# Turning activations to features with in-place 32x32 transposes and SBUF-to-SBUF DMAs, in three more places instead of TensorE

## The reference

```
h = h + concat(sgu, shortconv, conformer, pool of rms(h) @ w_in) @ w_out
h = h + (silu(rms(h) @ w_gate) * (rms(h) @ w_up)) @ w_down      # 2048 -> 5632 -> 2048
h = h + sigmoid(rms(h) @ w_ple_gate) * (p @ w_ple_proj)
x = rms(h, final)
q, k, v, gate = split(rms(x) @ swa_w_in)                        # 32 query heads, 4 key heads of 64
o = attention with window 128, bias table and sinks, after a norm of q and k
out = x + (o * silu(gate)) @ swa_w_out
```

## Time and profile before

| what | us |
|---|---|
| median of 3 runs | 1449.11 (1448.94 to 1449.32) |
| the profiled execution's own time | 1450.04 |
| its span | 1448.1 |
| TensorE matmul busy | 1441.9 (6655 instructions) |
| DVE busy | 981.4 |
| ScalarE busy | 697.1 |
| GpSimd busy | 50.4 |
| DMA traffic | 274.03 MB, mean 189 GB/s |

### The profile page before, as it was taken

One profiled execution on the slowest core, in us unless ns is written; L12 is line 12 of the kernel. 1 busy time (PEld: TensorE's weight loads), 2 busy tenths in 40 slices (PEclk: granted clock), 3 DMA queues, 4 the chain that ended last, 5 costly groups with the idle time before them and its releaser, 6 DMA issues.

```text
span 1448.1 us, 18176 instructions
## 1 busy us (share of the span) xinstructions
PE 1441.9 (100%) x6655; PEld 1194.7 (83%) x6655; DVE 981.4 (68%) x1364; ACT 697.1 (48%) x924; POOL 50.4 (3%) x52
## 2 busy tenths in 40 slices
PE   9999999999999999999999999999999999999999
PEld 7888888888888888888888888888888888888887
DVE  5599977886666654566765546769798567665553
ACT  7444564554444433444443344445555566564432
POOL 2000010000000000000000000000000212200000
PEclk9999999999999999999999999999999999999999
DMA  9665556566665556666555666655565745444462
GB/s 332 220 189 175 175 184 220 192 191 190 201 192 197 191 191 197 193 190 195 193 190 192 198 190 194 196 185 179 191 203 175 236 155 171 151 127 163 171 207 88
DMA packets 141495, 274.03 MB, mean 189 GB/s; under 512 B 8594, under 2 KB 10894, under 8 KB 141305
## 3 DMA queue, kind: packets, MB, share of 16 engines
q1 hardware_dynamic: 139608, 266.49, 56.7%
q0 software_dynamic: 1792, 6.71, 1.5%
q10 hardware_dynamic: 32, 0.01, 0.0%
HBM read 271.02 MB, written 2.15 MB: 189 GB/s over the span
## 4 chain that ended last, share of the span: by engine, by line
PE 97%; DVE 1%; ACT 1%; DMA 0%; issue 0%; ACTq 0%
PE acc L1264 31%; PE acc L1266 30%; PE acc L1265 30%; PE tp L1506 1%; PE acc L1326 1%; PE tp L1284 1%; PE sp L1487 1%; PE tp L1294 1%; DVE w_lo L777 1%; DVE tile L1141 0%; ACT tile L701 0%; DMA resid<-in_x 0%; ACT w_hi L480 0%; DVE smx L1145 0%; PE tp L1316 0%
## 5 line engine op out<-in xcount | busy, mean ns | idle before, releaser
L777 DVE TENSOR_TENSOR w_lo<-w_raw,w_hi 128x1024 fp32r<-128x1024 f32 x500 | 610.6, 1225 | 400.3 <-ACT w_hi L480 397.6
L480 ACT ACTIVATE w_hi<-w_raw 128x1024 fp32r<-128x1024 f32 x500 | 528.1, 1059 | 604.4 <-PE acc L1266 603.6
L1264 PE MATMUL acc<-w_lo,yh 128*128 128x512 f32 x1184 | 461.5, 390 | 0.0
L1266 PE MATMUL acc<-w_hi,yl 128*128 128x512 f32 x1184 | 460.7, 389 | 0.0
L1265 PE MATMUL acc<-w_hi,yh 128*128 128x512 f32 x1184 | 460.6, 389 | 0.0
L1264 PE MATMUL acc<-w_lo,hh 128*128 128x512 f32 x784 | 309.5, 395 | 0.0
L1266 PE MATMUL acc<-w_hi,hl 128*128 128x512 f32 x784 | 305.7, 390 | 0.0
L1265 PE MATMUL acc<-w_hi,hh 128*128 128x512 f32 x784 | 305.1, 389 | 0.0
L1264 PEld LDWEIGHTS acc<-w_lo,yh 128*128 128x128 f32 x1184 | 222.3, 188 | 46.8 <-issue 0.6
L1266 PEld LDWEIGHTS acc<-w_hi,yl 128*128 128x128 f32 x1184 | 222.2, 188 | 46.0
L1265 PEld LDWEIGHTS acc<-w_hi,yh 128*128 128x128 f32 x1184 | 222.3, 188 | 45.9
(11 more groups left out here) (150 smaller groups left out, 555.7 us busy)
## 6 DMA issues: line engine op xcount, KB each, us to landing
w_raw<-in_w_gate SPq DMA_DIRECT2D x88, 512.0 KB, 4.2
w_raw<-in_w_up SPq DMA_DIRECT2D x88, 512.0 KB, 4.4
w_raw<-in_w_down SPq DMA_DIRECT2D x88, 512.0 KB, 4.1
w_raw<-in_swa_w_in SPq DMA_DIRECT2D x72, 512.0 KB, 3.6
w_raw<-in_w_in SPq DMA_DIRECT2D x64, 512.0 KB, 4.2
w_raw<-in_w_out SPq DMA_DIRECT2D x32, 512.0 KB, 4.1
w_raw<-in_w_ple_gate SPq DMA_DIRECT2D x32, 512.0 KB, 3.5
w_raw<-in_swa_w_out SPq DMA_DIRECT2D x32, 512.0 KB, 3.6
```

Source lines behind the costliest of these rows:

```text
L480: act.activation(w_hi[:, s % SPL], w_raw[:, s % RAW], ACT.Copy).then_inc(hi_ready, 1)
L777: dve.tensor_tensor(w_lo[:, s % SPL], w_raw[:, s % RAW], w_hi[:, s % SPL].bitcast(F32), ALU.subtract).then_inc(lo_ready, 1)
L1264: pe.matmul(dst, xh[:, f, tk], w_lo[:, s % SPL, k], start=(f == 0), stop=False)
L1266: last = pe.matmul(dst, xl[:, f, tk], w_hi[:, s % SPL, k], start=False, stop=(f == CK * n - 1))
```

## The change

The DVE transposes now stay on their own partitions: two instructions of 128 partitions by 512 elements turn all 32x32 blocks of a stretch inside each partition quarter. Then SP issues 16 DMAs of 32 partitions by 1 KB from SBUF to SBUF, one for each pair of source quarter q and target quarter r. `turned` is now counted by these DMAs, and `blocks_done` tells SP that the blocks are turned. The halves read the result through a view with four dimensions, by token half. All 20 turns are made so, and six more that TensorE made: the keys (T_K), the gated output (T_OG, four) and the third stretch of the last down input (T_HID + 10). turned_high and turned_low come one step later than before in the loops (step 10 for 9), the last down stage gets an order TAIL and the output projection the order DOWN.

```diff
+TAIL = [(0, c) for c in range(4)] + [(1, c) for c in range(4)] + [(0, 4), (0, 5), (1, 4), (1, 5)]
+TAIL += [(d, c) for d in (2, 3) for c in range(6)]
...
+T_FFN, T_HID, T_PLE, T_SWA, T_K, T_OG = 0, 4, 15, 18, 21, 22
...
+        def turn_buffers(n):
+            if n < T_PLE or T_SWA <= n < T_K:
+                return tile[2][:], tile[3][:]
+            if n < T_SWA:
+                i = 2 * ((n - T_PLE) % 2)
+                return tile[2 + i][:], tile[3 + i][:]
+            if n == T_K:
+                return wide[:, 0, 1024:], wide[:, 1, 1024:]
+            i = (n - T_OG) % 2
+            return tile[(5, 3)[i]][:], tile[(4, 2)[i]][:]
+
+        def turned_tile(n):
+            return turn_buffers(n)[1].rearrange("p (q k t n) -> p k t q n", q=4, k=4, t=T)
+
+        def quarters(dst):
+            return dst.rearrange("p k (t q n) -> p k t q n", t=T, q=4)
...
+            def move(n, lap=ONCE, freed=None):
+                sp_.wait_ge(blocks_done, n + 1 + lap.turns)
+                if freed is not None:
+                    sp_.wait_ge(turned, 256 * n)
+                    sp_.wait_ge(turned_lo, low_count(freed))
+                src, dst = turn_buffers(n)
+                for q in range(4):
+                    for r in range(4):
+                        sp_.dma_start(dst[32 * r:32 * (r + 1), 256 * q:256 * (q + 1)],
+                                      src[32 * q:32 * (q + 1), 256 * r:256 * (r + 1)]).then_inc(turned, 16)
...
+                    if n is not None and c == 5:
+                        move(n, lap)
...
+            for n, (d, c) in enumerate(TAIL):
+                load(START[base + 4] + n, wd_v, 2 * KT + CK * c, CW * d)
+                if n == 12:
+                    move(T_HID + 10)
+                if n == 22:
+                    move(T_PLE)
...
+                    if (j, c) == (3, 2):
+                        move(T_K)
+                    if j >= 7 and c == 5:
+                        move(T_OG + j - 7)
...
-                act.wait_ge(turned, n + 1 + lap.turns)
+                act.wait_ge(turned, 256 * (n + 1) + 256 * lap.turns)
+                src, dst = turned_tile(n), quarters(dst)
                 if gains is None:
-                    last = act.activation(dst, feat(TURN), ACT.Copy)
+                    for t in range(T):
+                        last = act.activation(dst[:, :, t], src[:, :, t], ACT.Copy)
...
+            def keys():
+                act.wait_ge(turned, 256 * (T_K + 1))
+                for t in range(T):
+                    last = act.activation(quarters(feat(3))[:, :, t], turned_tile(T_K)[:, :, t], ACT.Copy)
+                last.then_inc(turned_hi, 1)
...
-            def turn(src, quarters, done=False):
-
-                for q in quarters:
-                    for r in range(4):
-                        block = src[P // 4 * q:P // 4 * (q + 1)].rearrange("p t (k r n) -> p t k r n", k=4, r=4)[:, :, :, r]
-                        into = feat(TURN)[P // 4 * r:P // 4 * (r + 1)].rearrange(
-                            "p k (t q n) -> p t k q n", t=T, q=4)[:, :, :, q]
-                        last = dve.transpose(into, block)
+            def turn(n, src):
+
+                into = turn_buffers(n)[0].rearrange("p (r k t n) -> p k r t n", r=4, k=4, t=T)
+                for t in range(T):
+                    block = src[:, t].rearrange("p (k r n) -> p k r n", k=4, r=4)
+                    last = dve.transpose(into[:, :, :, t], block)
+                last.then_inc(blocks_done, 1)
...
                     for k in range(4):
+                        for t in range(T):
+                            last = dve.scalar_tensor_tensor(dst[:, k, t], src[:, k, t], gains[:, k:k + 1], hi[:, k, t],
+                                                            ALU.mult, ALU.subtract)
...
-                    if (j, c) == (0, 1):
+                    if (j, c) == (0, 3):
                         ple_turned_low(2)
...
+            def turn_gated(g):
+
+                dve.wait_ge(og_ready, g + 1)
+                turn(T_OG + g, wide[:, :, CW * g:CW * (g + 1)])
...
+                    if (v, c) == (2, 2):
+                        turn(T_K, tok(2))
...
+                    if c == 5 and v >= 6:
+                        turn_gated(v - 6)
...
+            for n, (d, c) in enumerate(TAIL):
+                if n == 0:
+                    pe.wait_ge(turned_lo, T_HID + 10)
+                if n == 8:
+                    pe.wait_ge(turned_lo, T_HID + 11)
+                chunk(START[base + 4] + n, base + 4 + d, c, hh, hl)
...
+                if n == 0:
+                    pe.wait_ge(turned_hi, T_K + 1)
...
-                    if c == 5 and v >= 6:
-                        pe.wait_ge(og_ready, v - 5)
-                        g = v - 6
-                        to_features(H_OG[g], wide[:, :, CW * g:CW * (g + 1)])
...
+            for n, (d, c) in enumerate(DOWN):
+                if d == 0 and c in (0, 2, 4, 6):
+                    pe.wait_ge(turned_lo, low_count(T_OG + c // 2))
+                chunk(START[SO_UNIT] + n, SO_UNIT + d, c, yh, yl, by_bank=last_bank if n == len(DOWN) - 1 else None)
```

More of the change, by code:

```diff
@@ L399, in _ @@
                     load(START[PLE_UNIT + j] + c, wpg_v, CK * c, CW * j)
+                    if (j, c) == (0, 0):
+                        move(T_PLE + 1, freed=T_PLE - 1)
+                    if (j, c) == (0, 6):
+                        move(T_PLE + 2, freed=T_PLE)
+                    if j >= 2 and c == 4:
+                        move(T_SWA + j - 2)
             for j, col in enumerate(SWA_ORDER):
@@ L628, in pair @@
                         square(1, 3)
-                    if first and c == 8:
+                    if first and c == 9:
                         ffn_turned_high(3)
-                    if kt is not None and c == 9:
+                    if kt is not None and c == 10:
                         turned_high(T_HID, hh[:, bass.ds(kt, 4)], None, lap)
@@ L659, in _ @@
                         take(base, tok(0), ACT.Silu, rf, lap)
[L660 to L669, removed]
+            for n in range(len(TAIL)):
+                split(START[base + 4] + n)
+                if n == 9:
+                    turned_high(T_HID + 10, hh[:, 8:12])
+                if n in (14, 16, 22):
+                    d = (14, 16, 22).index(n)
+                    wait_left(act, base + 4 + d)
+                    square(2, d)
+                if n in (19, 22):
+                    ple_turned_high((19, 22).index(n))
             rp = rs[:, R_PLE]
@@ L726, in _ @@
                     if (v, c) == (2, 6):
-                        copy(H_K, tile[3])
+                        keys()
                     if c == 0 and 3 <= v <= 6:
                         copy(H_Q[v - 3], tile[4], gqk[:, 0:1])
-                    if c == 0 and v >= 7:
-                        high(H_OG[v - 7], yh[:, 4 * (v - 7):4 * (v - 7) + 4])
+                    if c == 2 and v >= 7:
+                        turned_high(T_OG + v - 7, yh[:, 4 * (v - 7):4 * (v - 7) + 4])
                     if c == 2 and 4 <= v <= 7:
@@ L750, in _ @@
                         copy(H_PT[v - 3, 1], tile[7])
-            for j in range(NG):
-                for c in range(8):
-                    split(START[SO_UNIT + j] + c)
-                    if (j, c) == (0, 0):
-                        high(H_OG[2], yh[:, 8:12])
-                    if (j, c) == (0, 3):
-                        act.wait_ge(og_ready, 3)
-                        take(SO_UNIT - 1, tok(1), ACT.Silu, rr)
-                    if (j, c) == (0, 5):
-                        high(H_OG[3], yh[:, 12:16])
+            for n in range(len(DOWN)):
+                split(START[SO_UNIT] + n)
+                if n == 2:
+                    turned_high(T_OG + 2, yh[:, 8:12])
+                if n == 3:
+                    act.wait_ge(og_ready, 3)
+                    take(SO_UNIT - 1, tok(1), ACT.Silu, rr)
+                if n == 9:
+                    turned_high(T_OG + 3, yh[:, 12:16])
         @block.vector
```

195 lines of the change are left out of this document (81 added, 114 removed).

## The result

The change made the kernel slower: median 1453.0 us (1452.46 to 1456.55, 7 runs) against 1449.05 (7 runs of the kernel before on the same chip), a ratio of 1.0032, 95% interval 1.002 to 1.0043. The forecast was 1443.7.

What follows compares the result with a forecast made beforehand. TensorE, busy 1441.9 of 1448.1 us, was taken as the bound. Removing six to_features gave -5.4 and everything else 0: 1450.04 to 1444.6 us profiled, 1443.7 against the median 1449.11; range 1442.8 to 1446.5.

Steps and rivals of the forecast that it cites:

- Six blocks, -5.4: TensorE: six to_features calls of eight transposes removed, 0.87 us each; bounds 5.2 to 5.6, taken as 5.4 us.
- I take the quicker row and a little for the gap to the next, 0.30: 4.8 us a move: SP's issuing of 16 DMAs per move: 0.30 us each, from a small load's 0.25 us without backlog.
- Limits 11.0 and 17.0: Landing after the turn: beyond 11.0 us ScalarE stalls, at 17.0 TensorE stops, counting 5.5 us of cover ahead of TensorE.
- What is queued behind on SP: SP's next weight load is delayed 3.4 us by a move, with 15 us spare, so nothing is lost.
- (b), 6.3 of 8.2: PLE: the residual sum its transposes need now stands behind ple_turned_low(2), about 6.3 us of 8.2; nothing added.
- (a), turn_gated: Attention group 3: turn_gated(0), 1.3 us, precedes DVE's emptying of a bank, 1.4 us available; stall at most 0.1.
- thin places give some back: Rival: 1 to 4 us lost in attention, the keys or last down input, 1445 to 1448 us; chance 0.09.
- The first rival: Moves land too late, ScalarE then TensorE wait; decides from 0.79 us per DMA; about 1526 us at 1.0; chance 0.08.
- The copies slow the matmuls: Rival at TensorE: 5% slower matmuls while 26 x 512 KB pass, 2.3 us; no separate chance given.
- lane groups one after another: Rival on DVE: the four lane groups run in sequence, a 7.0 us turn, 1449 to 1475 us; chance 0.03.
- one by one: Rival: each DMA completes before the next begins, 33.6 us a move, about 1840 us; chance 0.02.
- Signs of being wrong: turned_high waits over 5 us, SP's DMAs over 0.5, a transpose over 1, or w_lo releasing TensorE in steady stages.

Runs made afterwards that it cites:

- the run with 32 DMAs: Changed kernel with each of a move's 16 DMAs cut in two, for the FFN and hidden inputs only: 1578.68 us (one run).
- the kernel with everything moved: Changed kernel, add_resid before the low half, attention inputs' halves at step 2, keys turned two steps earlier, all 16 DMAs kept: 1443.83 us, ratio 0.9963.

## Why the prediction was wrong

- *Six blocks, -5.4:* right. -5.4 to -5.6 in the ledger of every kernel that removes six.
- *The turn, 1.3 us:* right, two of 0.69. *More work on DVE and ScalarE inside the cover:* right for TensorE in the FFN; DVE fell to 881.2 us.
- *"I take the quicker row and a little for the gap to the next, 0.30: 4.8 us a move":* this step failed. An issue takes 0.59 us, 0.627 with the gap, 10.0 us a move. The earlier trace rows gave 0.25, 0.72 and 1.54, of which I took the lowest, by an argument on the load of the DMA engines. But 0.25 was for a parameter vector of 2 KB. The trace of before also had 500 weight loads, in the FFN and everywhere else, and SP takes 0.37 us to issue one, so the issues differ by kind and 0.30 lay below the commonest kind (kernel before, ns):

```profile
L356 SPq DMA_DIRECT2D w_raw<-in_w_up x88: 368/373/373, 286.2 to 919.9; - x88
```

No row of before had the 0.59 of an SBUF-to-SBUF DMA, and no run shows why it is 0.59 and not 0.37. The landing, 2.1 to 4.4 us behind the last issue, was too high in turn: it is 1.25. A move takes 11.3 us and not 7 to 9.

- *Limits 11.0 and 17.0:* right where they were worked out, at the hidden inputs of the FFN, as the run with 32 DMAs shows. There 11.3 costs nothing, and at the FFN inputs, where 17.0 was 1 to 3 us too high, it costs nothing either. *The failed half of this step is that I used them elsewhere.* At the attention's inputs the turn comes later in its step and the limit of ScalarE is 7.4, and the 5.5 us of cover, read at one chunk of the last down stage, are 4.8 and less there and 0.3 to 0.8 at chunks 403 to 405, as the trace of before showed. For the keys ScalarE's limit was 6.9 and not 8.3, and I gave 14 for TensorE's side, with the scores in mind; what stopped TensorE stands further down the row, in the group where the earlier trace rows showed TensorE waiting already, 0.42 us, with no cover left.
- *What is queued behind on SP:* I looked at the loads behind a move, rightly harmless, and not at the move behind a move. The second PLE turn ends 5.4 us after the first (987.51), and SP is at the first move until 992.1; the second begins at 994.15, 6.6 us after its turn, and the third 4.0 after its own.
- *(b), 6.3 of 8.2:* the sum was fine for a move that is on time, with 1.9 us to spare. The move was 4.2 late, so 2.3 would be lost, and 2.6 were.
- *(a), turn_gated:* right, no step at group 3.
- *Rivals:* "thin places give some back", 1 to 4 us, with the note that issues of 0.55 us would already cost, was the mechanism, at a chance of 0.09. The steps come to 9.1 us with the clock, more than it allowed, because four places were hit and a stop slows the clock. The first rival, late moves everywhere, did not decide: the 0.627 us from issue to issue is under its threshold of 0.79.
- *The copies slow the matmuls, lane groups one after another, one by one:* refuted by the kernel with everything moved at 1443.83, by 0.69 us a transpose, and by 1.25 us behind the last issue.
- *Signs of being wrong:* of the four that were given, one came, SP's DMAs at over 0.5 us. ScalarE's longest wait for a move was 4.8 us, under the 5 named, and that was enough to stop TensorE.

## What to carry over

Count the issuing engine's time for each small DMA, here 0.59 us for 16 or for 32 KB (the kernel's 512 KB loads take 0.37), and compare issue x count, plus the move it may stand behind, with the slack at each place of use, not at the typical one. Where one issuer is the limit and another engine idles, sharing the issues halved the time of the late moves and gave back all 9 us; so did an order with the residual sum first, the attention inputs' halves a step later and the keys two steps earlier. And a stop of some 2 us in a saturated TensorE can cost more than twice its length, since the clock may drop behind it: the same stop of 1.75 us cost 2.3 to 4.8.

## What the runs showed that I had not expected

- An SBUF-to-SBUF DMA of 16 or 32 KB takes SP 0.59 us to issue in all three shapes tried, and GpSimd 0.50 us (4.03 us for eight). It lands 1.8 us after the start of its issue, and the next doesn't wait for it.
- The slow clock after a stop is not settled by the stop's length as these rows show it: 2.4 us at 1022 was followed by full clock, 2.6 us at the same place in another kernel by 0.59, 1.75 us at 1191 by 0.72, and stops of 1.74 and 1.75 us at that same place in two other kernels by 1.0 and 0.51. Kernels with a stop of some 1.75 us or more had runs 1.4 to 4.1 us apart, and their mean granted clock went from 1.0 or 0.999 in the fastest run of each to 0.999 to 0.996 in the slowest. Kernels with no step over 1.2 us in attention and none over 0.4 in PLE had runs 0.4 to 0.9 apart, all at 1.0; the one with steps of 1.2 and 1.8 us in attention, 1.8. Why the clock falls behind one stop and not behind the other stays open.
